# A mixture-of-experts slot table built by one-hot matrix products and a running sum, in place of scatters to memory

## The reference

```python
def hier_moe(h, w_rg, b_rg, w_re, b_re, w1, w3, w2):
    ...
    g_val, g_idx = lax.top_k(g_logit, 1)
    ...
    e_val, e_idx = lax.top_k(e_logit, TOP_K)
    gates = p_group[:, None] * jax.nn.softmax(e_val, axis=-1)
    expert = g_idx * EXP_PER_GROUP + e_idx
    ...
    dest = pstarts[se] + jnp.arange(a) - starts[se]
    ...
    slot_tok = jnp.zeros(n_blocks * MOE_BLOCK, jnp.int32).at[dest].set((order // TOP_K).astype(jnp.int32))
    slot_gate = jnp.zeros(n_blocks * MOE_BLOCK, h.dtype).at[dest].set(flat_g[order].astype(h.dtype))
    block_e = jnp.minimum(jnp.searchsorted(pends, jnp.arange(n_blocks) * MOE_BLOCK, side='right'),
                          N_EXPERTS - 1)
    ...
        return (jax.nn.silu(xb @ w1[e]) * (xb @ w3[e])) @ w2[e]
```

## Time and profile before

| | before |
|---|---|
| median of 3 runs | 3268.12 us (3266.55 to 3270.43) |
| the profiled execution, its own time | 3271.28 us |
| its span, first to last instruction | 3269.3 us |
| mean granted clock of PE | 0.92 of full speed |
| PE busy | 2780.4 us (85%) |
| DVE busy | 1135.8 us (35%) |
| ACT busy | 459.1 us (14%) |
| POOL busy | 328.3 us (10%) |
| chain that ended last | PE 69%, DMA 15%, DVE 6%, issue 4%, SPq 4%, ACT 2%, POOL 1% |

### The profile page before, as it was taken

How to read it: one execution, slowest core, us unless ns; L and a number is a source line. 1 busy time by engine, 2 the same in 40 slices (tenths; PEclk the granted TensorE clock), 3 DMA queues, 4 the chain that set the end, 5 groups by cost and what they waited for, 6 DMA issues and landing times.

```text
span 3269.3 us, 33809 instructions
## 1 busy us (share of the span) xinstructions
PE 2780.4 (85%) x11690; PEld 1288.1 (39%) x11690; DVE 1135.8 (35%) x2171; ACT 459.1 (14%) x848; POOL 328.3 (10%) x460
## 2 busy tenths in 40 slices
PE   6999969999999999897599877866999488997783
PEld 3444424444444465555233322324565233332221
DVE  4989950320021222645321111127254421211114
ACT  2111130100110102511000000001151000100000
POOL 0110021000000000002311111110000311111110
PEclk9999989999999999997799988987989699999996
DMA  6665521222211210014499999973102598479994
GB/s 207 207 206 167 169 89 53 93 77 77 77 52 62 77 52 26 1 47 161 159 334 322 387 386 383 348 259 141 52 1 91 216 373 305 138 279 392 386 362 176
DMA packets 271498, 604.21 MB, mean 185 GB/s; under 512 B 18756, under 2 KB 43653, under 8 KB 270016
## 3 DMA queue, kind: packets, MB, share of 16 engines
q1 hardware_dynamic: 255872, 581.75, 49.3%
q0 software_dynamic: 15552, 21.47, 2.3%
HBM read 740.27 MB, written 29.60 MB: 235 GB/s over the span
## 4 chain that ended last, share of the span: by engine, by line
PE 69%; DMA 15%; DVE 6%; issue 4%; SPq 4%; ACT 2%; POOL 1%; DVEq 0%; POOLq 0%; ACTq 0%
DMA arena<-in_w 14%; PE psum L1253 13%; PE psum L925 10%; PE psum L974 10%; PE psum L1102 9%; PE psum L946 7%; PE psum L1276 4%; PE psum L1197 4%; SPq L584 3%; PE psum L1149 2%; PE psum L1138 2%; PE psum L910 1%; PE psum L995 1%; PE psum L1212 1%; PE psum L1161 1%
## 5 line engine op out<-in xcount | busy, mean ns | idle before, releaser
L1253 PE MATMUL psum<-arena 128*64 128x512 f32 x2688 | 663.1, 650 | 169.9 <-DMA arena<-in_w 118.7
L1253 PEld LDWEIGHTS psum<-arena 128*64 128x64 f32 x2688 | 222.8, 149 | 599.2 <-issue 551.0
L925 PE MATMUL psum<-arena 128*128 128x512 f32 x768 | 345.2, 603 | 2.8 <-ACT arena L656 2.8
L974 PE MATMUL psum<-arena 128*128 128x512 f32 x768 | 329.9, 592 | 0.8 <-ACT arena L648 0.8
L1276 PE MATMUL psum<-arena 128*64 128x512 f32 x1344 | 311.5, 605 | 15.3 <-DVE arena L1895 11.0
L1352 DVE SCALAR_TENSOR_TENSOR arena<-arena 128x512 f32<-128x512 f32 x464 | 308.8, 748 | 0.0
L1895 DVE COPY arena<-psum 128x256 f32<-128x256 f32 x84 | 35.5, 425 | 766.0 <-PE psum L1264 760.8
L1102 PE MATMUL psum<-arena 128*128 128x512 f32 (+1 forms) x800 | 288.3, 522 | 5.9 <-issue 4.0
L946 PE MATMUL psum<-arena 128*128 128x512 f32 x512 | 225.2, 603 | 11.1 <-POOL arena L1988 10.4
L974 PEld LDWEIGHTS psum<-arena 128*128 128x128 f32 x768 | 145.8, 190 | 184.2 <-issue 183.2
L925 PEld LDWEIGHTS psum<-arena 128*128 128x128 f32 x768 | 143.0, 191 | 174.9 <-issue 174.9
(11 more groups left out here) (265 smaller groups left out, 2157.5 us busy)
## 6 DMA issues: line engine op xcount, KB each, us to landing
arena<-in_w SPq DMA_DIRECT2D x260, 2048.0 KB
arena<-in_w_ada SPq DMA_DIRECT2D x48, 1024.0 KB, 5.1
arena<-in_conv_w_in SPq DMA_DIRECT2D x24, 1024.0 KB
arena<-in_ret_w_in SPq DMA_DIRECT2D x12, 2048.0 KB, 8.0
arena<-in_w_in SPq DMA_DIRECT2D x8, 2048.0 KB, 8.2
arena<-moe_out SPq DMA_DIRECT2D x10, 1024.0 KB, 9.3
arena<-in_conv_w_out SPq DMA_DIRECT2D x4, 2048.0 KB, 10.3
arena<-in_ret_w_out SPq DMA_DIRECT2D x4, 2048.0 KB, 7.8
```

The source lines that it names most:

```text
L925: m = pe.matmul(bank(b + c), w[:, k, c * P:(c + 1) * P], c_hT[:, k, :], start=(k == 0), stop=(k == KD - 1))
L974: m = pe.matmul(bank(4 * (n % 2) + j), l_, r_, start=(k == 0), stop=(k == KD - 1))
L1253: m = pe.matmul(bank(4 * s)[part], m_xsT[s][:, k, :], m_w[s][j][:, k, :], start=(k == 0), stop=(k == KD - 1))
```

## The change

The table is no longer in memory. The slot `dest` of each token and choice is split into a block `hi` and a position `lo`. For each tile and choice VectorE writes a one-hot row of the position (64 columns), once times the row number less 4096 and once times the gate (`posw`, 128 columns), and a one-hot row of the block (`blk`, 82 columns in layer 0 and 66 in layer 1). PE multiplies the transposed `posw` with `blk` and adds up over tiles and choices, 12 or 8 products, in bank 6: partitions 0 to 63 then hold the row number of each slot of each block, partitions 64 to 127 the gate. An empty slot gets 0 and, with 4096 added back, a row outside the tokens. VectorE copies the parts straight into `g_idx` and `g_slot_gate`. Both choices are made one after the other, so that PE has the first half while VectorE writes the second.

The first blocks of the experts come from a running sum along 16 experts, one for the even and one for the odd ones, and `lower` isn't loaded. The expert of each block is found with one block to a partition, written into two columns (`g_cols`), and PE turns these into rows. GpSimd issues the first two gathers before it waits for `meta`.

```diff
--- before.py
+++ after.py
...
+    t[:, T_I:T_I + 82] = np.arange(82)
+    row = 2 * (i[:, None, None] + P * np.arange(T)[None, None, :]) + np.arange(2)[None, :, None]
+    t[:, T_ROW:T_ROW + 2 * T] = row.reshape(P, 2 * T) - NO_ROW
+    t[:, T_P] = i
+    for l, n in enumerate((S + C, S)):
+        t[:, T_EXP + l] = np.where(i > E // 2 + 2 * n // SB, 1 - E, 0)
...
-                sp.dma_start(mem(o_r, E * E), a["lower"]).then_inc(sem("wr"), 16)
...
                 pe.wait_ge(sem("rt_M"), past("rt_M", l) + 1)
-                pe.wait_ge(sem("tok0"), past("tok0", l) + 16)
+                pe.wait_ge(sem("ones"), past("ones", l) + 1)
                 M, before = mem(g_a[4], E * nt), mem(g_a[5], E * (nt + 1))
                 pe.matmul(bank(5, E * nt), tri, M, start=True, stop=False)
                 pe.matmul(bank(5, E * nt), g_ones, before[:, 0:E * nt], start=False, stop=True)
                 pe.matmul(bank(5, E, E * nt), g_ones, before[:, E * nt:E * nt + E], start=True, stop=True)\
                     .then_inc(sem("rank"), 1)
+                nr = NR[l]
+                posw, blk = mem3(g_posw, 2 * nt, 2 * SB), mem3(g_blk, 2 * nt, nr)
+                for k in range(2):
+                    pe.wait_ge(sem("dest"), past("dest", l) + k + 1)
+                    for j in range(nt * k, nt * (k + 1)):
+                        m = pe.matmul(bank(6, nr), posw[:, j, :], blk[:, j, :], start=(j == 0), stop=(j == 2 * nt - 1))
+                m.then_inc(sem("rank"), 1)
+                pe.wait_ge(sem("dest"), past("dest", l) + 3)
+                for o in range(2):
+                    m = pe.transpose(psum[0:1, 7 * 512 + P * o:7 * 512 + P * o + nr], g_cols[0:nr, o:o + 1],
+                                     ident[0:nr, 0:nr])
+                m.then_inc(sem("rank"), 1)
+
                 pe.wait_ge(sem("idx"), past("idx", l) + 1)
-                nr = NR[l]
-                for o in range(3):
-                    column = g_rowf[0:nr, :, o] if o < 2 else g_rowsf[0:nr, :, 2]
-                    m = pe.transpose(psum[0:SB, 6 * 512 + nr * o:6 * 512 + nr * (o + 1)], column, ident[0:nr, 0:nr])
-                m.then_inc(sem("rank"), 1)
-
-                pe.wait_ge(sem("idx"), past("idx", l) + 2)
                 pe.wait_ge(sem("meta"), past("meta", l) + 1)
...
-                ids = g_ids.rearrange("p (t k) o -> p t k o", k=2)
...
-                link(dve.reciprocal(idsf[:, 0:nt, 0, 2], den))
-                link(dve.tensor_tensor(idsf[:, 0:nt, 1, 2], idsf[:, 0:nt, 0, 2], ed, ALU.mult))
-                dve.sem_inc(sem("dest"), 1)
+                link(dve.reciprocal(g_gate[:, 0:nt], den))
+                link(dve.tensor_tensor(g_gate[:, nt:2 * nt], g_gate[:, 0:nt], ed, ALU.mult))
 
                 dve.wait_ge(sem("rank"), past("rank", l) + 1)
                 link(dve.tensor_scalar(cnt, bank(5, E, E * nt), float(SB) / 2 - 0.5, 1.0 / SB, ALU.add, ALU.mult))
                 link(dve.tensor_copy(nb.bitcast(I32), cnt))
                 link(dve.tensor_copy(cnt, nb.bitcast(I32)))
                 link(dve.tensor_scalar(nb, cnt, 1.0, None, ALU.max))
-                link(dve.tensor_tensor(g_prod, g_lower, nb.unsqueeze(1).to_broadcast([P, E, E]), ALU.mult))
-                link(dve.tensor_reduce(pst, g_prod, AX.X, ALU.add))
-                link(dve.tensor_tensor(pend, pst, nb, ALU.add))
-                link(dve.tensor_tensor(cnt, pst, mem(TAB + T_OFF + E * l, E), ALU.add))
+                dve.wait_ge(sem("ones"), past("ones", l) + 1)
+                nbl = NBS[l] + 1
+                for s in range(2):
+                    mine, ends = (v.rearrange("p (j two) -> p two j", two=2)[:, s, :] for v in (nb, pend))
+                    link(dve.tensor_tensor_scan(ends, g_ones[:, 0:E // 2], mine, float(nbl * s), ALU.mult, ALU.add))
+                link(dve.tensor_tensor(pst, pend, nb, ALU.subtract))
 
                 offs = cand
-                link(dve.scalar_tensor_tensor(out=offs, in0=cnt.unsqueeze(1).to_broadcast([P, nt, E]),
+                link(dve.scalar_tensor_tensor(out=offs, in0=pst.unsqueeze(1).to_broadcast([P, nt, E]),
                                               scalar=float(SB), in1=bank(5, E * nt).rearrange("p (t e) -> p t e", t=nt),
                                               op0=ALU.mult, op1=ALU.add))
                 for k_, oh in enumerate((oh1, oh2)):
                     link(dve.tensor_tensor(oh, oh, offs, ALU.mult))
-                    link(dve.tensor_reduce(i1, oh, AX.X, ALU.add))
-                    dve.tensor_copy(g_dest[k_][:, 0:nt], i1).then_inc(sem("dest"), 1)
-                    dve.wait_ge(sem("dest"), past("dest", l) + k_ + 2)
-
-                nbl, half_e = NBS[l] + 1, E // 2
...
-                    link(dve.tensor_copy(g_new[0:1, s * nbl:(s + 1) * nbl], first))
-                link(dve.tensor_reduce(be[0:1, 0:1], pend[0:1, E - 2:E], AX.X, ALU.max))
+                    link(dve.tensor_reduce(g_dst[:, nt * k_:nt * (k_ + 1)], oh, AX.X, ALU.add))
+
+                nr = NR[l]
+                dst, hi, hi_i, lo = (v[:, 0:2 * nt] for v in (g_dst, g_hi, g_hi_i, g_lo))
+                link(dve.tensor_scalar(hi, dst, 1.0 / SB, 0.5 / SB - 0.5, ALU.mult, ALU.add))
+                link(dve.tensor_copy(hi_i, hi))
+                link(dve.tensor_copy(hi, hi_i))
+                link(dve.scalar_tensor_tensor(out=lo, in0=hi, scalar=-float(SB), in1=dst, op0=ALU.mult, op1=ALU.add))
+                posw, blk = mem3(g_posw, 2 * nt, 2 * SB), mem3(g_blk, 2 * nt, nr)
+                for k_ in range(2):
+                    js = slice(nt * k_, nt * (k_ + 1))
+                    pos = g_pos[:, js, :]
+                    link(dve.tensor_tensor(pos, iota[:, 0:SB].unsqueeze(1).to_broadcast([P, nt, SB]),
+                                           over(lo[:, js], nt, SB), ALU.is_equal))
+                    link(dve.tensor_tensor(posw[:, js, 0:SB], pos,
+                                           over(mem(TAB + T_ROW + T * k_, nt), nt, SB), ALU.mult))
+                    link(dve.tensor_tensor(posw[:, js, SB:2 * SB], pos, over(g_gate[:, js], nt, SB), ALU.mult))
+                    dve.tensor_tensor(blk[:, js, :], iota[:, 0:nr].unsqueeze(1).to_broadcast([P, nt, nr]),
+                                      over(hi[:, js], nt, nr), ALU.is_equal).then_inc(sem("dest"), 1)
+                    dve.wait_ge(sem("dest"), past("dest", l) + k_ + 1)
+
+                place, expert, fresh = mem(TAB + T_P, 1)[0:nr], g_cols[0:nr, 0:1], g_cols[0:nr, 1:2]
+                cmp = cand[0:nr, 0, :]
+                link(dve.tensor_scalar(cmp, pend[0:nr], place, None, ALU.is_le))
+                link(dve.tensor_reduce(expert, cmp, AX.X, ALU.add))
+                link(dve.tensor_scalar(expert, expert, 2.0, mem(TAB + T_EXP + l, 1)[0:nr], ALU.mult, ALU.add))
+                link(dve.tensor_scalar(expert, expert, float(E - 1), None, ALU.min))
+                link(dve.tensor_scalar(cmp, pst[0:nr], place, None, ALU.is_equal))
+                dve.tensor_reduce(fresh, cmp, AX.X, ALU.add).then_inc(sem("dest"), 1)
+                link(dve.tensor_scalar(be[0:1, 0:1], pend[0:1, E - 1:E], -float(nbl), None, ALU.add))
+                link(dve.tensor_tensor(be[0:1, 0:1], be[0:1, 0:1], pend[0:1, E - 2:E - 1], ALU.max))
                 link(dve.tensor_scalar(g_n[l][0:1, 0:1], be[0:1, 0:1], -2.0, None, ALU.add))
+
+                dve.wait_ge(sem("rank"), past("rank", l) + 2)
+                slots = bank(6, nr)
+                link(dve.tensor_scalar(g_tok[:, 0:nr], slots[0:SB], 0.5, NO_ROW / 2 - 0.25, ALU.mult, ALU.add))
+                link(dve.tensor_copy(g_idx[:, 0, 0:nr], g_tok[:, 0:nr]))
+                link(dve.tensor_scalar(g_idx[:, 1, 0:nr], slots[0:SB], float(NO_ROW), None, ALU.add))
+                dve.tensor_copy(g_slot_gate[:, 0:nr], slots[SB:P]).then_inc(sem("idx"), 1)
+
+                dve.wait_ge(sem("rank"), past("rank", l) + 3)
+                link(dve.tensor_copy(g_be[0:1, 0:nr], psum[0:1, 7 * 512:7 * 512 + nr]))
+                link(dve.tensor_copy(g_new[0:1, 0:nr], psum[0:1, 7 * 512 + P:7 * 512 + P + nr]))
                 dve.sem_inc(sem("meta"), 1)
-
-                nr = NR[l]
-                dve.wait_ge(sem("tok0"), past("tok0", l) + 32)
-                dve.tensor_copy(g_rowf[0:nr], g_rows[0:nr, :, 0:2]).then_inc(sem("idx"), 1)
-                dve.wait_ge(sem("rank"), past("rank", l) + 2)
-                turned_rows = psum[0:SB, 6 * 512:6 * 512 + 3 * nr].rearrange("p (o n) -> p o n", o=3)
-                link(dve.tensor_copy(g_idx[:, :, 0:nr], turned_rows[:, 0:2, :]))
-                dve.tensor_copy(g_slot_gate[:, 0:nr], turned_rows[:, 2, :]).then_inc(sem("idx"), 1)
 
                 last = last_blocks(dve, l)
...
-                link(pool.memset(g_init[:, :, 0:2], 4096))
-                link(pool.memset(g_init[:, :, 2], 0))
-                link(pool.memset(g_ones, 1.0))
-                pool.dma_start(slot_tok[l].rearrange("(p n) o -> p n o", n=nr // 2), g_init[:, 0:nr // 2, :])\
```

(23 more changed lines are left out.)

69 lines of the change are left out of this document (19 added, 50 removed).

## The result

| | before | changed |
|---|---|---|
| median of four launches, us | 3267.34 | 3239.55 |
| ratio, 95% interval | | 0.9908 [0.9891, 0.9926] |
| profiled execution, us | 3271.28 | 3238.72 |
| its span, us | 3269.3 | 3236.9 |

One launch of the changed kernel was disturbed (7298.3 us); the ratio leaves it out, the median of four does not, and the median of the other three is 3238.72. The change makes the kernel 0.9% faster, and the forecast was 3239.5. The profile shows whether it came out for the reasons given.

A forecast was written before the change was run, and what follows sets the result against it. The chain from rank sums to gather index copy was taken as on the path, paid in full. Savings of 15.6 + 13.0 = 28.6 us took 3271.28 to 3242.7; less 3.16 for the median, 3239.5, range 3235 to 3246.

The forecast's parts named there:

- The scatters are on the path and the saving is paid in full: Both layers' routing: 20 scatters of about 0.96 us on the path; savings of 15.6 and 13.0 us counted in full.
- Given back in the expert loop: Rival: the expert loop would end on the weights' stream whatever its start, at 3268 us; chance 0.03.
- Layer 0, VectorE's part: Layer 0, from the start of the counts to VectorE's last comparison: 9.27 us.
- slower: Rival: broadcast operands slow sixteen VectorE operations; at 4.3 times the gain is gone, at six times 3282 us; chance 0.02.
- PE's tail: Slot products left behind VectorE: six in layer 0, 2.7 us at 0.434 each; four in layer 1, 1.74 + 0.08.
- The counts' start in layer 1: Layer 1, before the counts: four short VectorE operations go, so the counts start 0.32 us earlier.
- is idle anyway: GpSimd's two row clears move ahead of the rank work, where GpSimd was taken to be idle.
- Gather and landing: Behind the index copy: left as they are, 3.82 us for the second gather in layer 0, 2.06 in layer 1.
- The clock: New PE products stay at granted clock 0.50, 0.434 us each; full-clock rival 3232.2 us, chance 0.05.
- the row: Profile window 1510 to 1515: PE busy 5.00 of 5.00 us at granted clock 0.50, 16 instructions in 3.47 us.
- the rule that I had named beside it: Trainium skill's clock gate: activity lifts the slow clock; new products might cost 0.24 each, 1.9 us less over both layers.

The follow-up runs named there:

- double_scatter: The kernel before with each scatter issued twice, the second time into a spare table that nobody reads: 3292.77 us, ratio 1.0079.
- delay: The changed kernel with eight dead 128x1024 VectorE products in each layer's routing, ahead of the block numbers: 3259.12 us, ratio to the kernel before 0.9978.
- lower_back: The changed kernel with the masked 128x1024 product and reduction in place of the scans, and SP's load of `lower`: 3245.81 us, ratio to the kernel before 0.9936.
- serial: The changed kernel, but PE waits for both halves of the one-hot rows before its first slot product: 3244.11 us, ratio to the kernel before 0.9928.
- quarters: The changed kernel with the one-hot rows in four groups in place of two: 3244.07 us, ratio to the kernel before 0.9931.
- clears: The changed kernel with GpSimd's two clears of the gather tiles behind VectorE's sum of the one-hot rows: 3238.87 us, ratio to the kernel before 0.9904.
- the later run: The changed kernel measured once more, unchanged: 3237.35 us, ratio to the kernel before 0.9906.
- filler: The changed kernel with five dead 128x512 PE products while PE waits for the gathers: 3238.9 us, ratio to the kernel before 0.9907.
- warm: The changed kernel with dead 512-column PE products behind the rank products (four, three) and slot products (three each): 3236.04 us, ratio to the kernel before 0.9905.
- pe_order: The changed kernel with side 1's first transposes on PE behind side 0's first expert products: 3240.33 us, ratio to the kernel before 0.9919.
- best: The changed kernel with `clears`, `warm` and `pe_order` in one: 3237.49 us, ratio to the kernel before 0.9902.

## Why the prediction was right, step by step

- *The scatters are on the path and the saving is paid in full.* Right. `double_scatter` adds 24.98 us to the fronts and 26.66 to the median beside it (3266.11), and `delay` puts 10.08 and 10.07 us back and finds 19.57 at the end. "Given back in the expert loop" is refuted.
- *Layer 0, VectorE's part.* The forecast 9.27 from the counts to the last comparison was 9.25 in the profile (the last comparison began 8.58 behind the counts and took 0.67). Scans of 16 elements cost 0.20, and `lower_back` confirms what they replace, 2.3 us. Broadcast operands cost nothing: 384 columns 0.57, 492 columns 0.68. The "slower" rival falls with that.
- *PE's tail.* The price of a product was right: 0.427, with the weight load setting it, since 36, 66 and 82 columns cost the same. The term left out is the start and the end of a batch, 0.29 us. In the sum itself there is a slip of 0.1 besides: six products of 0.434 take 2.6 us, longer than VectorE's second group of 2.47, so by its own prices the twelve are one unbroken run and end at 12.1 behind the counts, not at 11.97. Measured it is 12.26. From there to the index copy it is 1.25 in place of 1.10, as VectorE begins 0.09 behind PE and the copies take longer. So c-i was 13.51 against 13.07; in layer 1 10.88 against 10.5. `serial` shows that the overlap is there, +2.48 and +1.69, and `quarters` that VectorE's block work is hidden by PE only just.
- *The counts' start in layer 1.* Wrong in sign: 0.32 earlier was forecast, r-c grew by 0.18 there and by 0.42 in layer 0. The step that failed is the one that moved GpSimd's clears to where GpSimd "is idle anyway". They are free for GpSimd, but VectorE's scaling stands still beside them. `clears` gives 0.33 a layer back. The forecast also let VectorE begin 0.03 behind PE's last rank product in layer 1, where 0.11 was measured.
- *Gather and landing.* i-p stayed, 8.24 and 6.36 against 8.14 and 6.35. `meta` and `lower` cost nothing that shows.
- *The clock.* The slot products did not lift it: 0.50 through 5.41 us of unbroken work, and the first groups took 8.45 and 9.09 us. So it went by the row and not by the rule that I had named beside it. The kernel before shows the same for longer. In this window of its trace PE has only products of 36 and 128 columns and not one gap:

```profile
1509.00:1520.00 11.00, 11.00 (x54) 11.00 (x54) 2.73 (x8) 3.01 (x8) 0.00 (x0) 0.50 1.04 403
```

  With 512 columns it can be lifted, as `filler` and `warm` show, but `warm` lost it again, in layer 0 behind the wait for the rows and in layer 1 in the slot products.

The misses are 0.44 + 0.38 in c-i, 0.42 + 0.50 in r-c and 0.10 + 0.01 in i-p. Their sum, 1.85, is the 1.75 us between 28.6 and 26.85 but for rounding in the forecast's terms. Yet the median fell by 27.8 (28.6 with the median of three) and, in the later run, by 31.8 (3269.17 to 3237.35); the profiled spans differ by 32.4. So the times carry 1 to 5.5 us beyond the fronts. It sits in loop 0, 953.33 before and 947.60 and 949.23 after; `double_scatter`, which also has the old table, has 951.87. But `pe_order` and `best` have 954, and the other runs of the changed kernel's kind lie between 946.6 and 951.9, so one profile each does not settle whether the loop gained anything. That stays open. The forecast met the median of four to 0.05 us and that of three to 0.8, closer than its steps did, and that is luck: the fronts gave 1.75 us less than counted, and something outside them, which I can't place, gave at least half as much.

## What to carry to other kernels

A table built by small indirect scatters cost GpSimd 1.25 us for each, and then a wait and a read-back; here comparisons on VectorE and twelve or eight one-hot products on PE built the same table of 5248 slots in layer 0, and the stretch fell from 28.70 to 13.51 us. A price read off a steady stream leaves out what a short batch pays once for its start and its end (0.29 us here). Read such a step in stretches from start to start: they repeat to 0.1 us where the whole time differs by several between runs. When work is split to overlap two engines, split only as far as the fixed cost of an operation allows (0.29 against 0.42 us for half the columns). An engine's idle time is a free place only if the work put there does not hold up a neighbour, and an earlier start counts only if the work behind it starts earlier as well.

## What the runs showed of the hardware

- A small fp32 product with a 128x128 weight load, two instructions, took 0.427 us at granted clock 0.50 with 36, 66 or 82 columns, and 0.22 at 1.00 with 82; a batch of twelve took 0.29 more than twelve times that.
- PE's granted clock stayed at 0.50, 1.2 GHz, through 5.41 us of unbroken products with 82 columns, and in the kernel before through 11 us of 36 and 128 columns. Under eight 512-column instructions (5.90 us) it rose to 2.4 GHz: the next six slot products took 1.57 us.
- In `warm` it stood at 1.00 through a wait of 3.75 us for a gather and fell about 0.5 us after it; in layer 1 it fell with no wait longer than 1.05.
- A GpSimd clear of 0.97 us held a 6-column VectorE scaling for 0.97 us. GpSimd sums of 2.34 us held two-input VectorE operations of 24 columns for 2.02 and 2.37 us; a reduction beside them took 0.18.
- A gather right behind another starts 0.31 us after it, one behind its own index copy 0.83 to 0.96 us after that.
